# The gate and up products of a mixture-of-experts block in two PSUM banks: 48 matmuls of 256 columns in the place of 24 of 512

## The reference

```python
def swiglu(h, wg, wu, wd):
    return (jax.nn.silu(h @ wg) * (h @ wu)) @ wd
```

## Time and profile before

| | us |
|---|---|
| median of 3 runs (3275.0 to 3280.47) | 3280.45 |
| the profiled execution's own time | 3270.5 |
| its span, first to last instruction | 3268.3 |
| TensorE busy with matmuls | 2897.1 (89%) |
| TensorE's weight loads | 2179.6 (67%) |
| VectorE busy | 2177.0 (67%) |
| ScalarE busy | 1703.9 (52%) |
| mean granted clock of TensorE, of full | 0.953 |

### The profile page before, as it was taken

The page is one execution under the profiler, slowest core; times in us unless marked ns, Lnnn a source line. Parts: engine busy times, 40 slices in busy tenths (PEclk is TensorE's granted clock), DMA queues, the critical chain, the costliest instruction groups (busy, mean ns, idle before and its releaser), DMA issues.

```text
span 3268.3 us, 61147 instructions
## 1 busy us (share of the span) xinstructions
PE 2897.1 (89%) x13157; PEld 2179.6 (67%) x13158; DVE 2177.0 (67%) x3447; ACT 1703.9 (52%) x2435; POOL 925.3 (28%) x788
## 2 busy tenths in 40 slices
PE   6789999999829999999989989999899999999883
PEld 2355555555517888878777768777787777787772
DVE  1146666666754466677777877777777786767774
ACT  0132333333214365566666666667666665656665
POOL 0001111111132233233433433334333333333231
PEclk9899999999959999999999999999999999999996
DMA  9611111111136488798988898888989898798886
GB/s 372 180 39 52 39 39 52 39 38 52 39 97 188 104 256 261 216 292 264 322 295 281 274 303 278 272 282 275 306 272 293 267 303 249 239 281 271 290 253 232
DMA packets 160691, 690.94 MB, mean 211 GB/s; under 512 B 34097, under 2 KB 35761, under 8 KB 110610
## 3 DMA queue, kind: packets, MB, share of 16 engines
q1 hardware_dynamic: 93634, 500.17, 41.3%
q0 software_dynamic: 66896, 189.34, 25.4%
HBM read 587.54 MB, written 141.19 MB: 223 GB/s over the span
## 4 chain that ended last, share of the span: by engine, by line
PE 59%; DMA 12%; DVE 12%; issue 9%; ACT 4%; DVEq 2%; SPq 1%; ACTq 1%; POOL 1%; POOLq 0%
PE PB L1079 12%; PE PB L1081 12%; PE PB L1080 12%; PE PB L992 9%; DMA acc_tab<-arena,rec 6%; DMA RAW<-in_w_up_e 4%; PE PB L962 4%; DVE WS L886 2%; PE PB L950 2%; ACT WS L577 2%; PE PB L1109 2%; DMA arena<-in_ada_b 2%; PE PB L1051 1%; PE PB L1017 1%; PE PB L976 1%
## 5 line engine op out<-in xcount | busy, mean ns | idle before, releaser
L886 DVE TENSOR_TENSOR WS<-RAW,WS (+1 forms) x774 | 902.7, 1221 | 89.4 <-ACT WS L577 89.2
L577 ACT CAST WS<-RAW (+1 forms) x774 | 760.1, 1053 | 116.0 <-DMA RAW<-in_w_up_e 64.7
L483 POOL DMA_INDIRECT acc_tab<-arena,rec x215 | 404.1, 1879 | 1244.4 <-DMA acc_tab<-arena,rec 855.0
L1079 PE MATMUL PB<-WS,XR 128*128 x1720 | 684.2, 398 | 18.1 <-issue 10.0
L1081 PE MATMUL PB<-WS,XR 128*128 x1720 | 675.6, 393 | 0.0
L1080 PE MATMUL PB<-WS,XR 128*128 x1720 | 674.4, 392 | 0.0
L1079 PE MATMUL PB<-WS,HR 128*128 x860 | 384.5, 447 | 33.1 <-DVE HR L920 32.8
L1079 PEld LDWEIGHTS PB<-WS,XR 128*128 128x128 f32 x1720 | 327.0, 190 | 119.0 <-issue 52.8
L916 DVE SCALAR_TENSOR_TENSOR arena<-PB,arena,G 128x512 f32<-128x512 f32 x430 | 302.5, 746 | 112.9 <-PE PB L1081 106.3
L1081 PEld LDWEIGHTS PB<-WS,XR 128*128 128x128 f32 x1720 | 325.4, 189 | 68.2
L1080 PEld LDWEIGHTS PB<-WS,XR 128*128 128x128 f32 x1720 | 326.4, 190 | 66.0
(11 more groups left out here) (238 smaller groups left out, 3251.8 us busy)
## 6 DMA issues: line engine op xcount, KB each, us to landing
RAW<-in_w_gate_e SPq DMA_DIRECT2D x128, 1024.0 KB
RAW<-in_w_up_e SPq DMA_DIRECT2D x128, 1024.0 KB
RAW<-in_w_down_e SPq DMA_DIRECT2D x128, 1024.0 KB
arena<-in_ada_w SPq DMA_DIRECT2D x12, 2048.0 KB, 13.0
arena<-in_x SPq DMA_DIRECT2D x32, 512.0 KB, 3.6
h_tab<-arena SPq DMA_DIRECT2D x17, 512.0 KB, 2.9
acc_tab<-arena SPq DMA_DIRECT2D x16, 512.0 KB, 2.6
out<-fa SPq DMA_DIRECT2D x16, 512.0 KB, 5.1
```

What stands on the lines that cost most here:

```text
L483: g.indirect_dma_start(acc_tab, bass.IndirectOffsetOnAxis(ap=rec[:, (n - 1) % UNROLL:(n - 1) % UNROLL + 1], axis=0), ys[(n - 1) % 2], None ...
L577: nc.scalar.copy(to, of).then_inc(s["a_hig" if k < 4 else "a_hid"], 1)
L886: last = V.tensor_tensor(lo, raw, hi, ALU.subtract)
L1079: mm(bank, hi[:, k, :], w(k, 0), start=(k == 0), stop=False)
```

## The change

The gate product goes first, as 24 matmuls of 256 columns into bank 0, which the expert stage did not use; it signals the new semaphore `gate_done`. The up product follows, again 24 matmuls of 256 columns, into bank 7, and signals `gu_done`. ScalarE's SiLU waits for `gate_done` and reads bank 0. VectorE's product waits for both SiLU and `gu_done`. The columns multiplied are the same in all; each stationary operand is now loaded once for 256 columns and not for 512.

```diff
@@ ScalarE
-                            act.wait_ge(s["gu_done"], b + 2)
-                            A_(eg, B[7][:, 0:F], ACT.Silu).then_inc(s["eg_done"], 1)
+                            act.wait_ge(s["gate_done"], b + 1)
+                            A_(eg, B[0][:, 0:F], ACT.Silu).then_inc(s["eg_done"], 1)
@@ VectorE
                             v.wait_ge(s["eg_done"], b + 1)
-                            V.tensor_tensor(hb, eg, B[7][:, F:2 * F], ALU.mult).then_inc(s["h_ready"], 1)
+                            v.wait_ge(s["gu_done"], b + 2)
+                            V.tensor_tensor(hb, eg, B[7][:, 0:F], ALU.mult).then_inc(s["h_ready"], 1)
@@ TensorE
-                            gu_w = lambda k, o: WS[:, bass.ds(at + o, GUW)].rearrange("p (a k n) -> p k a n", a=2, k=KD)[:, k]
-                            parts(B[7].rearrange("p (a n) -> p a n", a=2), xh, xl, gu_w, KD).then_inc(s["gu_done"], 1)
+                            half_w = lambda a: lambda k, o: WS[:, bass.ds(at + (o + a * GUW // 2 + k * F), F)]
+                            parts(B[0][:, 0:F], xh, xl, half_w(0), KD).then_inc(s["gate_done"], 1)
+                            parts(B[7][:, 0:F], xh, xl, half_w(1), KD).then_inc(s["gu_done"], 1)
```

More of the change, by code:

```diff
@@ L239, in build @@
             e_cnt e_nb e_off e_tab e_row e_thr
-            w_gu w_dn a_hig a_hid v_spg v_spd rec_got rec_tr rec_go rec_win xg_z xg_r0 xg_r1 xg_r2 xg_r3 xg_used gu_done eg_done h_ready hT_a hT_sb xgT_a xgT_v y_done y_v added
+            w_gu w_dn a_hig a_hid v_spg v_spd rec_got rec_tr rec_go rec_win xg_z xg_r0 xg_r1 xg_r2 xg_r3 xg_used gate_done gu_done eg_done h_ready hT_a hT_sb xgT_a xgT_v y_done y_v added
             f_in0 f_in1 f_in2 f_in3 f_in4 f_sq f_v f_ln f_y f_out f_st f_g f_go f_ch""".split()
```

## The result

The changed kernel takes 3309.42 us (median of 4 runs, 3305.55 to 3315.37) against 3277.72 us for the kernel before on the same chip (4 runs, 3270.26 to 3280.47): a ratio of 1.0102, with a 95% interval of 1.0083 to 1.0121. It is slower, by 27 to 40 us. The profiled execution took 3312.0 us, with a span of 3309.8, 41.5 us more than the span of before.

What follows compares the result with a forecast made beforehand. TensorE was taken to bound undisturbed blocks, with VectorE late in others; 134 blocks at 0.32 us, 43 us, less a tenth, gave +38 us: 3318 us against the median. Range 3272 to 3365, the forecast's own 3300 to 3335.

Steps and rivals of the forecast that it cites:

- SiLU earlier: ScalarE's SiLU starts in the middle of the gate/up product; nothing downstream moves, in either sort of block: 0.
- 48 for 24: Gate/up product: 256-column matmuls at 0.120 us take 5.76 us, 0.32 more a block; chance 0.42.
- Once per weight load: Gate/up matmuls: the 0.0134 us over the columns' time is added by something beside the array, for each stationary operand loaded.
- proportional surplus: Gate/up matmuls: extra time halves with the columns, 0.1135 to 0.115 us each, 0 to +11 us; chance 0.26.
- a bound by the weight load alone: Gate/up product: loads set the pace at 0.111 us, 0.11 us less a block, -15 us, 3265; chance 0.09.
- a shared reader: Gate/up matmuls: load and stream share a reader, 0.136 us each, 1.09 more a block, +146 us, 3426; chance 0.08.
- issue: Gate/up matmuls: instruction issue sets the pace at 0.124 us each, +68 us, 3348; chance 0.09.
- a refetched body: TensorE's longer loop body no longer fits and waits at each of 27 turns, +62 us, 3380; chance 0.06.
- Register instructions: Two of three gate/up matmuls have one ahead; issue takes at most 0.12 us a matmul, so 0 is added.
- the queue's lead: TensorE's queue, after the up product, has half the time per instruction in hand: 0, at most 0.2 us a block.
- The sum: Over the expert stage: 134 blocks pay 0.32 us, 43 us, less a tenth for late weights: +38 us.
- About 1.0 us of slower matmuls fit in there: Blocks where VectorE's product is late: a longer gate/up product is absorbed up to about 1.0 us, so they pay nothing.

Runs made afterwards that it cites:

- split_late_silu: The changed kernel with SiLU made to wait for the up product as well, as it did before the change; 3308.98 us, ratio 1.011.
- load_64: The kernel before, with only 64 of the 128 stationary columns loaded for each gate/up matmul; one run, 3279.08 us.
- extra_8: The kernel before with eight more 512-column matmuls ahead of each gate/up product, into unused bank 0, 1.81 us a block; 3514.47 us, ratio 1.0733.

## Why the prediction was right

- **The bound.** Right. TensorE is the bound in the undisturbed blocks, and their length followed the gate/up product (9.35 to 9.65 us). The block that I read, of 9.43 us, was not free of waits as I wrote: it lost 0.08 us at the start of its down product.
- **SiLU earlier: 0.** Right, and shown by `split_late_silu`. The step "VectorE's product then ends 0.42 us after the up product" was off: it is 0.62. I had counted the instruction's 0.42 us and left out the 0.20 from TensorE's last matmul to the start of what waits for it, which the earlier trace rows show for SiLU (1183.09 to 1183.29). With 1.67 us to spare it cost nothing.
- **48 for 24: 0.120 us each.** Right: 0.120. The term of 0.32 us a block measured 0.30 (5.744 against 5.445). That the surplus is per matmul, which I had taken from half clock and float32 rows, holds in the gate/up product for two widths: 0.227 at 512 and 0.120 at 256 columns, each 0.013 to 0.014 over the columns. At 384 columns the run in the down product doesn't bear it out. "Once per weight load" was my reading of what causes it, and is not shown; `load_64` shows that at 512 columns it doesn't shrink with the load's length. The Trainium skill's "TensorE: Matmul & The Clock Gate", section "Back-to-back issue gap", gives 109 ns for 256 columns by a formula that it calls the gap of an isolated matmul; by that rule the change would have been faster, and the measured 120 ns decides against it for this type.
- **The rivals.** In the gate/up product, proportional surplus and a bound by the weight load alone (0.1135 and 0.111) fall with 0.120; so do a shared reader (0.136) and issue (0.124, for which the earlier trace rows give only 0.12). The rival of a refetched body falls too: the second instruction queue moved 15 packets for 13. I had written that TensorE doesn't wait at "issue" as VectorE does, and that was wrong: its loads at the heads of blocks waited 88.5 us so in 103 cases. It is 81.8 us in 90 cases now, so the longer body added nothing there.
- **Register instructions and the queue's lead: 0.** Right. The down product starts 0.82 us after the up product, and 0.81 in undisturbed blocks before.
- **The sum.** I had 134 paying blocks at 0.32 us, less a tenth: 38 us. Measured are 35.2 us in the stage: 114 on-time blocks at 0.28 each, 32 us, 33 longer on-time blocks at 0.05, and next to nothing from the rest. So 38 came out close partly by luck. The 81 waits for line 907 are no count of late blocks, since only 53 were late by length, and 147 were on time; but 33 of these were longer than 9.49 us already and took in most of the 0.30. The tenth that I took off for late weights has no counterpart of its own in the traces.
- **"About 1.0 us of slower matmuls fit in there".** Right for 28 of the 53 late blocks, where 1.1 us fits (1.81 - 0.70), and the 0.30 us of the change is well inside it. But it was worked out from one late block, of 10.44 us, and 25 others are of another sort, 12.7 us long on the mean. 0.3 us a block could not reveal that, and `extra_8` did, where they became shorter. Lateness itself goes away once TensorE's turn is as long as VectorE's.

Open are what adds the 0.0134 us, why the down product's surplus is larger, why the longest late blocks became shorter as work was added, and why VectorE waits once in each turn of the loop.

## What to carry to other kernels

Before splitting a matmul by columns, read the distance between starts in an undisturbed stretch, take N over the clock from it, and charge what is left again for every new matmul: 24 more of them were 0.30 us a block. A long wait in front of an instruction is a gain only if someone waits for what that instruction makes; the 345.8 us in front of SiLU moved to the next instruction of ScalarE. To forecast how much of a lengthening shows, sort all blocks by their length and not by a count of waits, and price the slack of each sort by itself: here 55 to 62% showed, from 0.3 to 1.8 us a block, but as a sum of blocks that paid in full, blocks that paid what went beyond about 1.1 us, and blocks that became shorter.

## What the runs showed of the hardware

- Matmuls of this type with a new stationary operand each have a surplus over their columns at the full clock: in the gate/up product 13 to 14 ns at both 512 and 256 columns, in the down product 17 to 19 ns at 512 and 14 at 384, and none that can be seen at half clock. Halving the load's columns shortened its record to 0.14 us, by 0.05, and did not shorten the distance (0.230, from 0.227).
- At 128 columns a pair of load and matmul takes 0.110 us, about the same for fp32r matmuls and for the transposes (0.111), so the load probably sets the pace. By the Trainium skill, "TensorE: Matmul & The Clock Gate", section "LDWEIGHTS (loading the stationary operand)", a load takes its columns over 1.2 GHz, 107 ns for 128; the trace is 3 ns above that.
- Delaying two of VectorE's weight pieces by one turn, in the turns that carry most work, cost 8.4%: with weights that arrived late, much more than all the waits that it was to remove.
